# Leaving the empty slots out of the expert scatters of a two-block layer

## The reference

```python
    xs = h[tok]
    sizes = jnp.bincount(expert, length=N_EXPERTS).astype(jnp.int32)
    a = lax.ragged_dot(xs, w1, sizes)
    b = lax.ragged_dot(xs, w3, sizes)
    y = lax.ragged_dot(jax.nn.silu(a) * b, w2, sizes)
    y = (y * weights[order][:, None]).astype(h.dtype)
    return jax.ops.segment_sum(y, tok, num_segments=N)
...
        x = x + gt2 * y
```

## Time and profile before

| | |
|---|---|
| median of three runs | 3199.19 us |
| profiled execution, its own time | 3200.7 us |
| its span | 3198.8 us |
| PE busy over the span | 2780.3 us (87%) |
| DVE / ACT / POOL busy | 2194.5 / 1272.8 / 861.7 us |
| bytes moved by DMA | 552.78 MB, mean 173 GB/s |
| queue q1 (issued by SP) | 436.94 MB |
| queue q0 (issued by POOL) | 68.39 MB |

### The profile page before, as it was taken

One profiled execution on the slowest core, in us unless ns is written; L12 is line 12 of the kernel. 1 busy time (PEld: TensorE's weight loads), 2 busy tenths in 40 slices (PEclk: granted clock), 3 DMA queues, 4 the chain that ended last, 5 costly groups with the idle time before them and its releaser, 6 DMA issues. The chain is left out here.

```text
span 3198.8 us, 35725 instructions
## 1 busy us (share of the span) xinstructions
PE 2780.3 (87%) x13124; PEld 2220.8 (69%) x13124; DVE 2194.5 (69%) x2950; ACT 1272.8 (40%) x2069; POOL 861.7 (27%) x399
## 2 busy tenths in 40 slices
PE   6999999979588869879989968879599589999998
PEld 3777776755366658668777856768478478888786
DVE  5699975526698845844635978952444479888887
ACT  2222221120266621123224115656322067777775
POOL 1432210000111100001210025454321036776674
PEclk9999999989798989989999989989799689999999
DMA  6233347633455361235542245220532289999997
GB/s 217 95 105 116 106 159 256 204 123 132 157 182 187 139 246 51 88 80 132 122 119 67 85 119 101 52 50 17 220 114 105 112 305 389 385 383 384 384 381 240
DMA packets 244871, 552.78 MB, mean 173 GB/s; under 512 B 28949, under 2 KB 152325, under 8 KB 228434
## 3 DMA queue, kind: packets, MB, share of 16 engines
q1 hardware_dynamic: 174562, 436.94, 38.5%
q0 software_dynamic: 33840, 68.39, 8.8%
q10 hardware_dynamic: 36288, 45.09, 4.0%
HBM read 450.68 MB, written 108.59 MB: 175 GB/s over the span
## 5 line engine op out<-in xcount | busy, mean ns | idle before, releaser
L2549 DVE TENSOR_TENSOR e_low<-e_raw,e_high 128x4096 fp32r<-128x4096 f32 x99 | 439.5, 4441 | 81.7 <-ACT e_high L2543 81.6
L2543 ACT ACTIVATE e_high<-e_raw 128x4096 fp32r<-128x4096 f32 x99 | 359.6, 3635 | 115.9 <-DMA e_raw<-in_exp_w 88.8
L136 PE MATMUL banks<-h_high,w 128*128 128x512 f32 (+1 forms) x1088 | 308.5, 367 | 9.1 <-POOL w L365 4.4
L136 PE MATMUL banks<-p_w_high,p_high 128*128 128x512 f32 (+1 forms) x640 | 250.5, 391 | 14.7 <-DVE p_w_low L1594 14.7
L136 PE MATMUL banks<-p_w_high,p_low 128*128 128x512 f32 (+1 forms) x640 | 246.0, 384 | 0.0
L136 PE MATMUL banks<-p_w_low,p_high 128*128 128x512 f32 (+1 forms) x640 | 245.9, 384 | 0.0
L136 PE MATMUL banks<-e_high,e_xhigh 128*128 128x512 f32 x528 | 213.1, 404 | 18.3 <-issue 16.5
L136 PEld LDWEIGHTS banks<-h_high,w 128*128 128x128 f32 x1088 | 195.1, 190 | 48.5 <-POOL w L365 4.9
L496 DVE SCALAR_TENSOR_TENSOR acc<-img,taps,acc 128x1024 f32<-128x1024 f32 x160 | 209.8, 1311 | 5.7
L136 PE MATMUL banks<-e_high,e_xlow 128*128 128x512 f32 x528 | 208.3, 395 | 0.0
L136 PE MATMUL banks<-e_low,e_xhigh 128*128 128x512 f32 x528 | 207.7, 393 | 0.0
(11 more groups left out here) (502 smaller groups left out, 6590.9 us busy)
## 6 DMA issues: line engine op xcount, KB each, us to landing
e_raw<-in_exp_w SPq DMA_DIRECT2D x99, 2048.0 KB
s_sums<-cumT SPq DMA_DIRECT2D x32, 768.0 KB, 4.5
w_raw<-in_w_in SPq DMA_DIRECT2D x20, 1024.0 KB, 6.6
s_X<-xtok SPq DMA_DIRECT2D x19, 1024.0 KB, 6.0
p_raw<-in_w_in SPq DMA_DIRECT2D x18, 1024.0 KB, 6.8
xbcT<-res ACTq DMA_DIRECT2D x20, 640.0 KB, 2.9
xtok<-xt ACTq DMA_DIRECT2D x20, 640.0 KB, 4.1
w_raw<-in_ada_w SPq DMA_DIRECT2D x12, 1024.0 KB
```

The source lines that it names most:

```text
L136: last = pe.matmul(out, a, b, start=start and n == 0, stop=stop and n == len(pairs) - 1)
L2543: act.activation(self.high[p % HIGHS][:], self.raw[p % RAWS][:], ACT.Copy).then_inc(*self.high_done.up())
L2549: dve.tensor_tensor(self.low[p % HIGHS][:], self.raw[p % RAWS][:], self.high[p % HIGHS][:].bitcast(F32), ALU.subtract).then_inc(*self.low_ ...
```

## The change

The scatter gets the same bound as the gather, so ids above 1023 are left out of it. The 128 dummy rows, the memset, the clearing DMA and POOL's wait for it are removed, and the output tensor has 1024 rows.

```diff
-ROWS_OUT = SEQ + P
...
             pool.indirect_dma_start(out=dram["result"], out_offset=bass.IndirectOffsetOnAxis(ap=ids[:, m:m + 1].bitcast(U32), axis=0), in_=y[:, m % 2, :],
-                                    in_offset=None, compute_op=ALU.add).then_inc(*(scattered if m < FIXED else spill_scattered).up())
+                                    in_offset=None, bounds_check=SEQ - 1, oob_is_err=False, compute_op=ALU.add).then_inc(*(scattered if m < FIXED else spill_scattered).up())
...
-        nought, emptied, pads_cleared = s.sb("e_nought", [P, 256]), s.sem("e_emptied"), s.dma("e_pads_cleared")
...
-            sp.wait_ge(*emptied.at(1))
-            sp.dma_start(dram["result"][SEQ:ROWS_OUT, :].rearrange("p (c n) -> p c n", c=4), over(nought[:], 1, 4)).then_inc(*pads_cleared.up())
-
-        pool.memset(nought[:], 0.0).then_inc(*emptied.up())
...
-        pool.wait_ge(*pads_cleared.at(1))
...
-    dram["result"] = nc.dram_tensor("result", (ROWS_OUT, D), F32, kind="ExternalOutput").ap()
+    dram["result"] = nc.dram_tensor("result", (SEQ, D), F32, kind="ExternalOutput").ap()
...
-    return out[0:SEQ].reshape(1, SEQ, D)
+    return out.reshape(1, SEQ, D)
```

## The result

| | before | after |
|---|---|---|
| median of 20 runs | 3198.03 us | 3202.96 us |
| lowest to highest | 3193.54 to 3201.17 | 3196.25 to 3209.11 |
| profiled execution, its own time | 3200.7 us | 3206.26 us |
| its span | 3198.8 us | 3204.0 us |

The ratio is 1.0015 [1.0009, 1.0021]: the change costs some 5 us. That is less than the 0.2% that was called no change, but the interval excludes a gain. The forecast of 3196.1 us had the sign wrong, and 3202.96 lies above its range of 3188.0 to 3200.5.

A forecast was written before the change was run, and what follows sets the result against it. The last stage was taken as bound by weights arriving over unevenly loaded DMA engines. Gains of 1.6, 1.3 and 0.2 us sum to 3.1; against the median 3199.19 that gives 3196.1 us, range 3188 to 3200.5.

The forecast's parts named there:

- What bounds the kernel: Last stage, experts: 21 cycles of 18.56 us wait for raw weights, 9 went at TensorE's 17.77; 16.6 us could be won.
- The uneven split: Gathers in the expert cycle: real rows lie on half of the DMA engines; its sum misses 18.56 us by 0.06.
- the even split: Gathers in the expert cycle: real rows spread evenly over 16 engines, a cycle of 17.98 us, missing 18.56 by 0.58.
- The busy engines keep their load: Scatters in expert stage: engines with real rows lose only few-token tiles' empty slots; gain 1.6 us, bounds 0 and 1.7.
- The last scatter: End of the kernel: tile with 7 real rows, four rows' time saved, 1.3 us, between 0.33 and 2.3.
- Descriptors on POOL: POOL's scatter instruction: the bound's comparison per slot costs 0 to 1 us at the last scatter, taken as 0.
- Memset and clearing: Head of POOL's chain, last stage: removing the memset gains 0 to 0.46 us, taken as 0.2; clearing DMA nothing.
- A: Expert cycles: load is even, bytes count, the whole weight wait goes; 18.1 us less, 3181.1 us; chance 0.13.
- B: Expert cycles: left-out rows of an adding scatter cost 0.6 us each, 1.0 us more a cycle; 3229 us; chance 0.05.
- C: Scatters: empty slots are still transferred, or left-out rows cost what full ones do; 3199.0 us; chance 0.05.
- The signs listed: Profile after: q0 some 8.9 MB less; cycles 18.4 to 18.6 us; ACT waits some 80 us; last scatter within 2.2.
- Wrong if they exceed 18.6: Expert cycles in the profile after: above 18.6 us the prediction is wrong, assigned to B.

The follow-up runs named there:

- e12: The changed kernel with gathers taking all rows on partitions 0 to 95, empty slots left out on 96 to 127; 3195.96 us, ratio 0.9997 to the kernel before.
- e3: The kernel before, unbounded scatter, with the ranks of an expert's tokens spread over the DMA engines; 3179.00 us, ratio 0.9941 to the kernel before.
- e4: The changed kernel with the ranks of an expert's tokens spread over the DMA engines; 3177.29 us, ratio 0.9939 to the kernel before.
- e9: The kernel before with a scatter bound that leaves out only the empty slots on partitions 96 to 127; 3206.35 us, ratio 1.0026.
- e11: The kernel before with dummy rows reversed and a scatter bound leaving out only empty slots on partitions 0 to 63; 3198.61 us, ratio 0.9999.
- e7: The changed kernel with gathers of all 128 rows, empty slots fetching an unused row; 3193.12 us, ratio 0.9984 to the kernel before.
- e6: The kernel before with gathers of all 128 rows, empty slots fetching an unused row; 3193.81 us, ratio 0.9986 to the kernel before.
- e5: The kernel before with a bound on the scatter that leaves nothing out; 3197.58 us, ratio 0.9996 to the kernel before.
- e2: The kernel before without memset, clearing DMA and POOL's wait, scatter unchanged; 3195.12 us, ratio 0.9997 to the kernel before.

## Why the prediction was wrong

**What bounds the kernel: right.** The second part of the chain goes at the pace of the weights, and in the 12 experiments the stretch went with ACT's wait for them: 93.5 us and more where it is 556 us or longer, 85.1 and less where it is 550.5 or shorter, with e12 between in both.

**The uneven split: right, but in part by luck.** It was chosen for a sum that met 18.56 within 0.06 us, and that sum couldn't decide. For 410 GB/s the prediction gives the even split 18.4 us; redone, 6.29 MB / 410 GB/s + 2.62 + 0.59 is 18.55, as near to 18.56 as the uneven one at 426. The landings show the uneven split, e3 and e4 by removing it. The doubt was the DMA share of 1.01, and shares did overstate: the kernel after has 0.98, though eight engines have little but 24 packets of weights in a cycle of 18.86 us, 16.3 us at 681 ns.

**"The busy engines keep their load", so the cycle stays 18.56: this step failed.** They kept their packets, in number and size; the conclusion did not hold. The term was a gain of 1.6 us with bounds 0 and 1.7, and it measured a loss of 8.6. I had costed the light half's rows at nothing because that half has slack, which bounds what they cost from one side only. I never asked what the light engines do when they are relieved: they run further ahead, and the heavy ones land later. Even the bounds excluded it, because a sum of loads per engine treats engines as independent. They are not: e9 changes only what the light engines carry and costs 8 us. The gain itself, from the few slots that are left out on heavy engines, is what e11 has alone, and there the stretch is 549.98 us: nothing of the 1.6 is to be seen, though one profile tells little below 1 us.

**Why the heavy engines land later: shown in their packets, not explained.** Their weight packets are longer where the light engines are relieved, by about what the cycles grow. What lengthens them stays open. That all 16 engines carry weights at once isn't enough: of the weight packets in strings with real rows during which that is so, 26% are over 630 ns after, 23% in e9, 6% before and 1% in e3. Nor is it told why four scattered rows on a light engine (e9) don't help when eight gathered ones (e7) do, or why e6 with 616 ns has no faster pace than before.

**The last scatter: right**, 1.3 forecast. The tail is 1.6 us shorter, and from POOL's last instruction to the end it is 3204.0 - 3198.13 = 5.9 us against 7.8, 1.9 less. The four rows that I took as a mean were right by luck: two engines hold the seven rows, four and three. **Descriptors on POOL: right**, nothing (e5). **Memset and clearing:** 0.2 us forecast, under what e2 can tell.

**The rivals.** *A*, bytes count over all engines: wrong. 9 MB less cost 8.6 us, 9 MB more (e6) cost nothing. Its page in the Trainium skill, "DMA: Bandwidth & Descriptors", section "Anatomy of one DMA", has the cost follow the bytes over all engines; these runs disagree for a lopsided transfer. With the rows spread, fewer bytes land the weights sooner, after 10.6 us and not 14.1, but TensorE sets the pace there and the stretch doesn't show it. Its price for a kernel without the wait was near: 18.1 us less, and e4 has 3196.06 - 3177.29 = 18.8 us less. *B*, dear left-out packets: the right sign, the wrong mechanism. The packet of a left-out scatter slot takes 9 ns in the median of every kernel that has them, 14 in the mean at most (e9), not 0.47 us, and e4 has all of them at no loss. *C*: wrong by the bytes on q0.

**The signs listed.** Right: q0 8.90 MB less in as many packets; 9.51 MB in 5472 packets is 0.50 MB in 288; the last scatter's packets within 2.2 us (2.0, to the end of the last one); the DMA share at 0.98. Wrong: cycles of 18.86 instead of 18.4 to 18.6, ACT's wait 99 instead of 80 us. "Wrong if they exceed 18.6" was the right test, with the wrong name on it.

## What to carry to other kernels

When only some rows of an indirect DMA are real, ask which partitions they lie on before asking how many bytes they are: here the placement was worth 0.6% and the bytes less than nothing. A transfer that ends on its last engine was not made faster here by relieving the others, but slower, so fix the balance first, then trim. And where a bound on a term rests on slack, carry an end below zero unless something in the profile excludes it: here the engines that were relieved changed the timing of those that were not.

## What the runs showed of the hardware

- An adding scatter's row of 4 KB holds a DMA engine for 0.329 us, a gathered one for 0.159, both inside the stream of weights before; the 0.33 worked out from the lone scatter was right. A left-out slot is still a packet, of 4 bytes in a gather and 8 in a scatter, of 0.009 us in the median.
- These indirect DMAs spread over the engines by partition. A rank order that is even over them took the last landing of a 2 MB transfer from 16.4 to 14.1 us at the same bytes (e3), and to 10.6 without the empty slots (e4).
- Leaving out the empty slots of 32 of 128 partitions, all on the lightly loaded engines (e9), lengthens the mean cycle from 18.54 to 18.98 us, although those engines had slack with them and have more without. The weight packets of the other engines go from 626 to 639 ns in the mean.
